# Gated result transposed in x's banks, x's transposes one piece later, residual and MLP reads at later steps, four bank pairs in both output projections

## The reference

```python
h = h + mamba2_mixer(rms_norm(h, ssm_norm_w[0]), ...)     # w_in: 2048 -> z 4096, x 4096, B 1024, C 1024, dt 64
h = h + sq_relu_mlp(rms_norm(h, mlp_norm_w[0]), w_up[0], w_down[0])          # 2048 -> 8192 -> 2048
k, v = shared_kv(h, kv_norm_w, w_kv, k_norm_w)
h = h + diff_attention(rms_norm(h, attn_norm_w[0]), k, v, w_q[0], ..., w_o[0], lambda_init)
h = h + sq_relu_mlp(rms_norm(h, mlp_norm_w[1]), w_up[1], w_down[1])

def mamba2_mixer(h, ...):                     # 64 heads of 64 channels in 8 groups, state 128, chunks of 64
    z, xbc, dt = split(h @ w_in)
    xbc = silu(causal_depthwise_conv(xbc))    # four taps
    y = ssd_scan(x * dt, dt * a, B, C) + x * d_skip
    y = group_rms_norm(y * silu(z)) * out_norm_w
    return y @ w_out                          # 4096 -> 2048
def sq_relu_mlp(h, w_up, w_down):
    return square(relu(h @ w_up)) @ w_down
```

## Time and profile before

| | us |
|---|---|
| median of 3 runs (2512.79 to 2516.11) | 2513.65 |
| profiled execution | 2516.7 |
| its span | 2515.1 |
| PE busy | 2487.2 (99%), 11729 matmuls |
| PE weight loads busy | 2082.5 (83%) |
| DVE busy | 1526.3 (61%) |
| ACT busy | 1194.9 (48%) |
| POOL busy | 342.8 (14%) |
| DMA | 514.30 MB, 204 GB/s over the span |

### The profile page before, as it was taken

How to read it: one execution, slowest core, us unless ns; L and a number is a source line. 1 busy time by engine, 2 the same in 40 slices (tenths; PEclk the granted TensorE clock), 3 DMA queues, 4 the chain that set the end, 5 groups by cost and what they waited for, 6 DMA issues and landing times.

```text
span 2515.1 us, 32788 instructions
## 1 busy us (share of the span) xinstructions
PE 2487.2 (99%) x11729; PEld 2082.5 (83%) x11729; DVE 1526.3 (61%) x1552; ACT 1194.9 (48%) x1460; POOL 342.8 (14%) x335
## 2 busy tenths in 40 slices
PE   8999999999999999999999999999999999999999
PEld 7888888888888888888888788888888888888887
DVE  5777777775555556555555655656665465565554
ACT  5555555554444444444344545555544344444443
POOL 2422333330001001000011100001110010010010
PEclk9999999999999999999999999999999999999999
DMA  7565555555678677678677865554887686786785
GB/s 218 177 184 175 169 177 173 178 178 185 214 221 242 215 212 236 199 216 236 193 224 223 242 196 167 167 179 155 248 229 226 202 245 209 202 241 205 210 242 168
DMA packets 281381, 514.30 MB, mean 204 GB/s; under 512 B 20718, under 2 KB 53840, under 8 KB 280256
## 3 DMA queue, kind: packets, MB, share of 16 engines
q1 hardware_dynamic: 264736, 457.87, 59.2%
q0 software_dynamic: 16256, 54.94, 8.2%
q10 hardware_dynamic: 288, 0.11, 0.0%
HBM read 487.61 MB, written 25.23 MB: 204 GB/s over the span
## 4 chain that ended last, share of the span: by engine, by line
PE 56%; issue 28%; DMA 6%; DVE 4%; POOL 3%; ACT 2%; DVEq 0%; ACTq 0%; POOLq 0%; SPq 0%
PE acc L394 11%; PE acc L396 10%; PE acc L395 10%; PE aux L394 7%; PE aux L396 7%; PE aux L395 7%; DMA spread<-work 4%; DVE w_lo L1063 2%; POOL work L1563 2%; DMA work<-decay_rows 1%; PE aux L402 1%; POOL work L1528 1%; POOL work L1526 1%; DVE work L1150 1%; PE aux L463 1%
## 5 line engine op out<-in xcount | busy, mean ns | idle before, releaser
L1063 DVE TENSOR_TENSOR w_lo<-w_raw,w_hi 128x1024 fp32r<-128x1024 f32 x865 | 1117.9, 1302 | 794.5 <-ACT w_hi L712 792.2
L712 ACT ACTIVATE w_hi<-w_raw 128x1024 fp32r<-128x1024 f32 x865 | 911.2, 1059 | 1051.7 <-PE acc L396 588.7
L394 PE MATMUL acc<-w_hi,stationary 128*128 128x512 f32 x2176 | 854.5, 393 | 3.2 <-DVE w_lo L1063 2.0
L396 PE MATMUL acc<-w_hi,stationary 128*128 128x512 f32 x2176 | 847.5, 389 | 0.0
L395 PE MATMUL acc<-w_lo,stationary 128*128 128x512 f32 x2176 | 847.2, 389 | 0.0
L394 PE MATMUL aux<-w_hi,stationary 128*128 128x512 f32 (+1 forms) x1408 | 522.4, 371 | 7.0 <-DVE w_lo L1063 7.0
L396 PE MATMUL aux<-w_hi,stationary 128*128 128x512 f32 (+1 forms) x1408 | 520.6, 370 | 0.0
L395 PE MATMUL aux<-w_lo,stationary 128*128 128x512 f32 (+1 forms) x1408 | 520.6, 370 | 0.0
L394 PEld LDWEIGHTS acc<-w_hi,stationary 128*128 128x128 f32 x2176 | 408.7, 188 | 87.6 <-DVE w_lo L1063 1.7
L396 PEld LDWEIGHTS acc<-w_hi,stationary 128*128 128x128 f32 x2176 | 408.5, 188 | 85.6
L395 PEld LDWEIGHTS acc<-w_lo,stationary 128*128 128x128 f32 x2176 | 408.8, 188 | 82.9
(11 more groups left out here) (182 smaller groups left out, 1037.1 us busy)
## 6 DMA issues: line engine op xcount, KB each, us to landing
w_raw<-in_w_up SPq DMA_DIRECT2D x256, 512.0 KB
w_raw<-in_w_down SPq DMA_DIRECT2D x256, 512.0 KB
w_raw<-in_ssm_w_in SPq DMA_DIRECT2D x129, 512.0 KB
w_raw<-in_ssm_w_out SPq DMA_DIRECT2D x64, 512.0 KB
w_raw<-in_w_kv SPq DMA_DIRECT2D x64, 512.0 KB
spread<-work POOLq DMA_DIRECT2D x44, 512.0 KB, 3.7
work<-spread POOLq DMA_DIRECT2D x176, 128.0 KB, 5.9
w_raw<-in_ssm_w_in SPq DMA_DIRECT2D x64, 256.0 KB
```

Of the source, the lines that this page charges most:

```text
L394: pe.matmul(o, xh, hi[:, k], start=start, stop=False)
L396: mm = pe.matmul(o, xl, hi[:, k], start=False, stop=stop)
L712: a.activation(whi[:, s, :], raw[:, s, :], ACT.Copy).then_inc(sem("hi_made"), 1)
L1063: v.tensor_tensor(wlo[:, s, :], raw[:, s, :], whi[:, s, :].bitcast(F32), ALU.subtract).then_inc(sem("lo_made"), 1)
```

## The change

Gated transposes and their two splits use acc[0] in place of aux[0]. So a group's first piece waits for `cb_read` only, and `gate_lo` is waited for at piece 4, where acc[0] is written anew. x's transposes come after piece 14, not 13; the taps at step 18, the convolutions at 18 and 19, the exponential of m1 at 17. The output projection takes a mixed order and four bank pairs, its additions at 33, 35, 51 (before: 18, 34, 50), with the splits of the gated result at step 18 in place of 15. w_o's product uses four bank pairs and waits for no addition. Reads of the MLPs and additions come one or two steps later; the up projection's blocks 1 and 2 no longer wait for the addition of the last block.

```diff
+OUT_ORDER = ([(n, k) for n in (0, 1) for k in range(0, 28, 2)] + [(n, k) for n in (0, 1) for k in (28, 30)]
+             + [(n, k) for n in (2, 3) for k in range(0, 32, 2)])
-UPS = ((0, 7, 10, 17), (1, 15, 18, 25), (2, 23, 26, 33), (3, 31, 34, 41))
-UPS_FIRST = ((0, 13, 15, 23), (1, 15, 17, 26), (2, 23, 26, 33), (3, 31, 34, 41))
-DOWNS = ((0, 45, 47, 55), (1, 47, 49, 59), (2, 55, 58, None))
+UPS = ((0, 7, 11, 18), (1, 15, 19, 26), (2, 23, 27, 34), (3, 31, 35, 42))
+UPS_FIRST = ((0, 13, 17, 24), (1, 15, 19, 27), (2, 23, 27, 34), (3, 31, 35, 42))
+DOWNS = ((0, 45, 49, 57), (1, 47, 51, 61), (2, 55, 59, None))
+OUTS = ((0, 29, 33, 41), (1, 31, 35, 45), (2, 47, 51, None))
...
+        out_banks = (aux[0], acc[1], acc[0], aux[1])
...
-            with sp.Fori(0, 4) as n:
-                blocks(Pos(OUT0, n, 16), 0, ssm_w_out[0].rearrange("(k p) n -> p k n", p=P), n * NB, 16)
+            w_o0 = ssm_w_out[0].rearrange("(k p) n -> p k n", p=P)
+            for i, (n, kt) in enumerate(OUT_ORDER):
+                load(Pos(OUT0), i, (w_o0[:, kt:kt + 2, n * NB:(n + 1) * NB],))
...
-                transposes(to_channels(aux[0]), lambda i, t: gbuf[:, t, i * P:(i + 1) * P]).then_inc(sem("g_turned"), 1)
+                transposes(to_channels(acc[0]), lambda i, t: gbuf[:, t, i * P:(i + 1) * P]).then_inc(sem("g_turned"), 1)
...
                     if j == 0:
                         if not first:
-                            wait(pe, sem("gate_lo"), g - 1)
+                            pe.wait_ge(sem("cb_read"), g)
                     if j == 4 and not first:
                         pe.wait_ge(sem("x_read"), g)
+                        wait(pe, sem("gate_lo"), g - 1)
...
-                    if j == 13:
+                    if j == 14:
                         pe.wait_ge(sem("x_read"), g + 1)
...
                     if j == 15 and not first:
-                        pe.wait_ge(sem("cb_read"), g + 1)
                         turn_gated(g - 1)
...
+            for i, (n, kt) in enumerate(OUT_ORDER):
+                if i == 0:
+                    pe.wait_ge(sem("cb_read"), GROUPS)
+                if n == 0 and kt in (24, 28):
+                    pe.wait_ge(sem("gate_lo"), GROUPS - 1 if kt == 24 else GROUPS)
+                if n == 1 and kt == 0:
+                    pe.wait_ge(sem("z_read"), GROUPS)
+                if n == 3 and kt == 0:
+                    pe.wait_ge(sem("y_read"), GROUPS)
+                piece(Pos(OUT0), i, out_banks[n], NB, RB + kt, kt == 0, kt == 30)
+                if i == 2:
+                    turn_x_back(GROUPS - 1)
+                if i == 7:
+                    scan(GROUPS - 1)
+                if i == 14:
+                    pe.wait_ge(sem("x_read"), GROUPS)
+                    turn_gated(GROUPS - 1)
...
-                            pe.wait_ge(sem("resid_added"), R + 4 * c + u - 3 if c else R - 1 if u == 0 else R)
+                            pe.wait_ge(sem("resid_added"), R + 4 * c + u - 3 if c else R if u == 3 else R - 1)
...
-                if i == 16:
-                    pe.wait_ge(sem("resid_added"), R_WO + 1)
-                if i == 24:
-                    pe.wait_ge(sem("resid_added"), R_WO + 2)
-                piece(Pos(WO0), i, acc[n % 2], NB, RB + kt, kt == 0, kt == KT - 2)
+                piece(Pos(WO0), i, banks[n], NB, RB + kt, kt == 0, kt == KT - 2)
...
                     if j == 17:
+                        a.wait_ge(sem("masked"), g * 2 + 1)
+                        a.activation(m1, m1, ACT.Exp).then_inc(sem("decay_made"), 1)
+                    if j == 18:
                         a.wait_ge(sem("x_raw_turned"), g + 1)
...
-                    if j == 18:
-                        a.wait_ge(sem("masked"), g * 2 + 1)
-                        a.activation(m1, m1, ACT.Exp).then_inc(sem("decay_made"), 1)
...
-                    if first and i == 1:
+                    if first and i == 2:
                         resid_hi(2, T_MLP0_END + 3, to_att)
-                    if first and i == 3:
+                    if first and i == 4:
                         resid_squares(3, R_WO)
-                    if first and i == 9:
+                    if first and i == 10:
                         resid_hi(3, T_MLP0_END + 4, to_att)
...
-                    if j in (17, 18):
-
-                        conv_x(g, 2 * (j - 17))
+                    if j in (18, 19):
+
+                        conv_x(g, 2 * (j - 18))
```

More of the change, by code:

```diff
@@ L791, in tail @@
                     a.wait_ge(sem("g_turned"), r + 1)
-                    split_hi(aux[0], r * 4 + RB, r * 4 + N_OUT).then_inc(sem("gate_hi"), 1)
+                    split_hi(acc[0], r * 4 + RB, r * 4 + N_OUT).then_inc(sem("gate_hi"), 1)
             def read_x_product(dst, ps, n):
@@ L873, in _ @@
             to_mlp0, to_att, to_mlp1 = [(RA, N_MLP0)], [(RA, N_KV), (RC, N_ATT)], [(RA, N_MLP1)]
[L875 to L883, removed]
+            for i in range(len(OUT_ORDER)):
+                hi(Pos(OUT0), i)
+                tail(i, GROUPS - 1, 18)
+                for n, last, at_add, at_hi in OUTS:
+                    if i == at_add + 1:
+                        resid_squares(n, R_OUT + n + 1)
+                    if i == at_hi:
+                        resid_hi(n, T_OUT + n + 1, to_mlp0)
             def mlp(base, R, T, U, T_carry, before, after):
@@ L1199, in tail @@
                     v.wait_ge(sem("gate_hi"), r + 1)
-                    split_lo(aux[0], r * 4 + RB, r * 4 + N_OUT).then_inc(sem("gate_lo"), 1)
+                    split_lo(acc[0], r * 4 + RB, r * 4 + N_OUT).then_inc(sem("gate_lo"), 1)
             def group(g, first):
@@ L1226, in _, with add_resid @@
                 link.leave(GROUPS - 1)
-            def add_resid(n, pos, last, scaled, ps=None):
+            def add_resid(n, pos, last, scaled, ps):
                 v.wait_ge(sem("w_used"), pos.done(last))
                 hb = h[:, :, n * NB:(n + 1) * NB]
-                if ps is None:
-                    ps = acc[n % 2]
                 if not scaled:
@@ L1267, in _ @@
             to_mlp0, to_att, to_mlp1 = [(RA, N_MLP0)], [(RA, N_KV), (RC, N_ATT)], [(RA, N_MLP1)]
[L1269 to L1272, removed]
-                        tail(j, GROUPS - 1, 15)
-                    if n >= 1 and j == 2:
-                        add_resid(n - 1, Pos(OUT0), 16 * n - 1, False)
-                        turn_resid(n - 1, R_OUT + n, T_OUT + n)
-                    if n in (1, 2) and j == 8:
-                        resid_lo(n - 1, T_OUT + n, to_mlp0)
+            for i in range(len(OUT_ORDER)):
+                lo(Pos(OUT0), i)
+                tail(i, GROUPS - 1, 18)
+                for n, last, at_add, at_lo in OUTS:
+                    if i == at_add:
+                        add_resid(n, Pos(OUT0), last, False, out_banks[n])
+                        turn_resid(n, R_OUT + n + 1, T_OUT + n + 1)
+                    if i == at_lo:
+                        resid_lo(n, T_OUT + n + 1, to_mlp0)
             def mlp(base, R, T, U, T_carry, before, after, prev, squared):
@@ L1307, in chunk @@
                                 link(v.reciprocal(h_rs, h_ms))
[L1308 removed]
+                        elif j == 3:
                             add_resid(3, Pos(base, c, PER_CHUNK), -1, True, banks[3])
@@ L1388, in pair @@
                     lo(pos, i)
-                    if first and i == 1:
+                    if first and i == 2:
                         resid_lo(2, T_MLP0_END + 3, to_att)
-                    if first and i == 2:
+                    if first and i == 3:
                         add_resid(3, Pos(UP0, 3, PER_CHUNK), PER_CHUNK - 1, True, banks[3])
                         turn_resid(3, R_WO, T_MLP0_END + 4)
-                    if first and i == 9:
+                    if first and i == 10:
                         resid_lo(3, T_MLP0_END + 4, to_att)
@@ L1445, in _ @@
                     if 32 + i == at_add:
-                        add_resid(n, Pos(WO0), last - 32, False)
+                        add_resid(n, Pos(WO0), last - 32, False, banks[n])
                         turn_resid(n, R_WO + n + 1, T_WO + n + 1)
```

17 lines of the change are left out of this document (8 added, 9 removed).

## The result

The changed kernel takes 2530.32 us (median of 4, 2528.12 to 2532.34) against 2514.26 for the kernel before (four runs in the same session). The ratio is 1.0062, 95% interval 1.0051 to 1.0074: slower, by more than a measurement's uncertainty, and outside the forecast range of 2504 to 2515. The profiled execution took 2528.12, span 2526.5, so 11.4 us more span than before; the medians differ by 16.1, because the profiled execution is the fastest of its four, and the profiled one of before (2516.7) was slower than each of the four of before.

The account below looks back on a forecast made before the run. TensorE was taken to bound the kernel, so only its few waits count: 2516.7 - 4.4 (x's transposes) - 0.7 (output projection) - 1.1 (attention's entry) = 2510.5, with the median 3.05 lower, 2507.4 us; range 2503.8 to 2515.

Parts of the forecast that it names:

- The waits that the change removes: TensorE's waits for x's product in groups 1 to 7, 7 x 0.63 = 4.4 us, and one in the output projection, 0.7.
- Nothing moved in the MLPs: Additions and MLP reads one or two steps later: no wait of TensorE there, so 0 us.
- Group 0: First group: product for m0 and w_lo come within 0.2 us of each other; 0 or at worst +0.73, taken as 0.
- The chain to a group's end: From piece 16 to TensorE's next group: takes 9.12 us against 8.39 for three pieces; as long as before, everything 0.63 earlier.
- the 0.73: TensorE's wait at a group's end, put down to w_lo meeting GpSimd's m0 product; stays, seven times between groups, once into projection.
- Who goes next: After piece 16's w_lo: VectorE keeps its turn, m1 product waits for two w_lo; margin 0.1 us, saving 4.4 us.
- Rival 1: GpSimd's m1 product goes ahead of piece 17's w_lo: group ends +1.5 us each, 7 x 1.5 = 10.4, 2522.2 us; chance 0.1.
- The Trainium skill: Rule that the shared ports go to whichever was issued first; by it rival 1, 2522.2 us, would be the forecast.
- Attention's entry: Where the first MLP goes over into attention, 4.8 us idle: steps one later gain between 0 and 1.5 us, taken as 1.1.
- The range: Whole kernel: 2503.8 us with all of attention's idle time gone, up to 2515 over rival 2 (no change); rival 1 left out.

Follow-up runs that it names:

- run 1: Changed kernel with the exponential of m1 put back behind the taps, both at step 18: 2506.71 us, ratio to before 0.997.
- run 10: run 1's kernel with the exponential of m0 at step 5 of the tail in place of step 0: 2499.73 us, ratio to before 0.994.
- run 11: Changed kernel with the exponential of m0 at step 5 of the tail in place of step 0: 2500.04 us, ratio to before 0.9942.
- run 12: Kernel before with the exponential of m0 at step 5 of the tail in place of step 0: 2509.01 us, ratio to before 0.9978.
- run 2: Kernel before with only the exponential of m1 moved from step 18 to step 17, ahead of the taps: 2524.14 us, ratio to before 1.0038.
- run 4: Changed kernel with the exponential of m1 at step 18, still ahead of the taps: 2528.87 us, ratio to before 1.0059.
- run 7: Changed kernel with the group's x part and attention's entry steps (1, 2, 3, 9) as before, last-chunk additions late: 2510.36 us, ratio to before 0.9984.
- run 5: Changed kernel with 16 more matmuls of 256 columns, results unused, on TensorE at each group's start: 2523.22 us, ratio to before 1.0033.

## Why the prediction was wrong, point by point

- *The waits that the change removes.* Right in place and size: 7 x 0.63 and 0.74 are gone, in the changed kernel and in run 1. Nothing moved in the MLPs, as said. Group 0, taken at 0 with +0.73 at worst, came out at +0.5 in the changed kernel and +1.0 in run 1's first profile.
- *The chain to a group's end.* Right: from w_hi of the next piece 0 over the exponential and the product of m0 to the w_lo, the 0.73 stays as long as that product meets the w_lo. Runs 10 to 12 showed it by taking the meeting away: 5.6 us in the kernel before. The count in the prediction, and in the expectations of runs 10 and 12, is one too high: there are seven such ends and not eight, six between groups (0.73 each) and one into the projection (0.89), 5.3 together.
- *Who goes next.* This is the step that failed: "I take it that VectorE keeps going as long as its subtractions follow without a pause". It rested on one case, group 0, of the other, longer product. The m1 product goes between two w_lo (40 of 40), so the w_lo of piece 17 took 3.42 and not 1.21. The rest of the timetable was right, as run 1 shows by keeping the product out of it. Rival 1 had the mechanism and the durations: convolutions, tanh and w_hi about 2 us late, and a group's end of 1.5 us more. It came out as +1.3 each (1.95 more wait, 0.63 less at x's transposes), 9.1 for the 10.4 in its sum.
- *The Trainium skill.* "SBUF — State Buffer", Who interferes with whom: issue order decides. Runs 2 and 4 agree with it (product issued at 273.97, w_lo at 274.72, and the w_lo waits). Group 0 does not agree: in ten of the fourteen profiles its m0 product was issued while a w_lo ran, and in all ten it let two or three operations go first that were issued after it. In the changed kernel it was issued at 82.45, and a gate and a w_lo issued after it ran first (product to 89.78). Timelines of POOL and DVE:

```profile
82.45 7.33 POOL L1536 TENSOR_TENSOR work<-work 128x2048 f32<-128x2048 f32 x1 [6.93 <-ACT work L768]
```
```profile
82.33 1.22 DVE L1062 TENSOR_TENSOR w_lo<-w_raw,w_hi 128x1024 fp32r<-128x1024 f32 x1
83.46 0.69 DVE L1169 SCALAR_TENSOR_TENSOR work<-work 128x512 f32<-128x512 f32 x1
84.06 1.22 DVE L1062 TENSOR_TENSOR w_lo<-w_raw,w_hi 128x1024 fp32r<-128x1024 f32 x1
```

  Why the m0 product lets them pass and the m1 product doesn't stays open. The kernel before has one w_lo right behind another there too, so that is not it; the m0 product is twice as large (2048 elements per partition), and no run varied its size. With a rule on one side and a single place on the other, a chance of 0.1 for the rule was too small.
- *The clock.* Not in the forecast at all, nor in a rival: in the kernel before the clock did not fall after the 2.8 us at attention, which is why I priced waits by their length alone. I overlooked its one fall before the kernel's end, during the wait of 6.19 us at the launch. Half clock made up 8.6 of the profile's loss. Rival 1 with it would have been 2530.8, close to the measured 2530.32, but that is partly luck: between the two profiles the loss was 11.4, not the 17.2 of such a sum, since attention's entry gave 5.4 there and not 1.1.
- *Attention's entry.* The size was off: 1.1 forecast, 5.4 in the changed kernel's profile. How much of the 5.4 the change made is open: from piece 468 to 500 the nine profiles with the changed steps took 87.4 to 91.4 us, and the three with the old ones (before, runs 2 and 12) 91.3 to 93.0. It was also argued from the wrong steps (run 7).
- *The range* left out rival 1 by choice, and with it the time.

## What to carry to other kernels

Where two engines exclude each other, moving a request by one step decides between whose operations it falls; before moving it, list every operation of the other engine that it may meet, and don't take the order from a single place. A long operation of a side engine belongs where the path's engine has the most lead, not where its input happens to be ready: moving the m0 product there gave 5.6 us in the kernel before and made the changed kernel's harm harmless. A wait of TensorE costs what it lasts and can cost a stretch at half clock behind it: here waits of 2.7 to 3.0 us did in 14 cases of 19, 1.3 to 1.6 us each where I priced them.

## What the runs showed of the hardware

- After a wait TensorE's clock may fall to 0.50 for 3.4 us. Of the waits between 2.7 and 3.0 us from start to start in these profiles, 14 of 19 were followed by it; of the seven of 2.1 to 2.2 us in run 2, one; of the other waits under 2.3 us, none. The same wait with matmuls in it (run 5) left 0.95 at most to the next start and no fall. Length alone doesn't decide it: the wait at the launch, 4.9 to 7.0 us, was followed by half clock in nine of the fourteen profiles.
- A w_lo that waits for GpSimd ends 1.08 to 1.09 us after it, and a product of 1024 elements per partition that waits for a w_lo ends 2.25 to 2.27 after it, in all 40 cases.
- Two-input operations of VectorE that read PSUM (convolutions, splits) ran beside GpSimd's products without either getting longer: 2.41 for the product, 0.47 for each of the six.
